# Two transformer blocks in fp32 by split products: order of the odd mixer, weight splits ahead of the square, places of a shift product and of a skew store

## The reference, cut to what matters

```python
def odd_mixer(h, w_in, w_out, ..., glu_w):
    q, k, v, gate, u = jnp.split(h @ w_in, ...)
    r = retention(rotary(q), rotary(k), v)                 # 4 heads, decay by distance
    r = rmsnorm(r) * jax.nn.silu(gate)
    y = jax.nn.gelu(s5_ssm(u, ...))                        # a state space scan over time
    ga, gb = jnp.split(y @ glu_w, 2, axis=-1)
    y = ga * jax.nn.sigmoid(gb)
    return jnp.concatenate([r, y], axis=-1) @ w_out

def conv_ffn(h, w_in, conv_w, conv_b, w_out):
    val, gate = jnp.split(h @ w_in, 2, axis=-1)
    gate = causal_conv_of_3_taps(gate, conv_w) + conv_b
    return (jax.nn.gelu(gate) * val) @ w_out
```

## Time and profile before

| what | value |
|---|---|
| median of three runs | 3336.36 us |
| the profiled execution | 3337.56 us |
| its span in the trace | 3335.8 us |
| TensorE matmul busy | 3213.4 us, 96% of the span |
| VectorE, ScalarE, GpSimd busy | 1816.6, 1182.0, 1014.5 us |
| mean granted clock of TensorE | 0.986 |

### The profile page before, as it was taken

The page is one execution under the profiler, slowest core; times in us unless marked ns, Lnnn a source line. Parts: engine busy times, 40 slices in busy tenths (PEclk is TensorE's granted clock), DMA queues, the critical chain, the costliest instruction groups (busy, mean ns, idle before and its releaser), DMA issues.

```text
span 3335.8 us, 40175 instructions
## 1 busy us (share of the span) xinstructions
PE 3213.4 (96%) x14573; PEld 2571.0 (77%) x14573; DVE 1816.6 (54%) x2464; ACT 1182.0 (35%) x1787; POOL 1014.5 (30%) x722
## 2 busy tenths in 40 slices
PE   6999999999999999999999998999999999899998
PEld 5888866778888888866778887776788777778887
DVE  5454465565446443465555544445776767375443
ACT  3222244432223222345332222454433342343332
POOL 3994000059911810000069800000699000021000
PEclk9999999999999999999999999999999999999999
DMA  6664332156634633321156633211566344243332
GB/s 217 208 207 134 99 107 71 57 167 205 208 103 124 205 109 94 101 73 52 57 183 206 201 93 111 63 51 57 174 204 200 93 124 102 63 134 99 101 89 94
DMA packets 576073, 420.42 MB, mean 126 GB/s; under 512 B 29238, under 2 KB 536197, under 8 KB 574809
## 3 DMA queue, kind: packets, MB, share of 16 engines
q1 hardware_dynamic: 535332, 284.78, 29.0%
q0 software_dynamic: 35456, 124.01, 12.0%
q10 hardware_dynamic: 5172, 10.17, 0.9%
HBM read 413.10 MB, written 8.68 MB: 126 GB/s over the span
## 4 chain that ended last, share of the span: by engine, by line
PE 85%; DVE 9%; ACT 3%; issue 1%; DMA 1%; ACTq 0%; SPq 0%; DVEq 0%
PE bank L326 25%; PE bank L328 24%; PE bank L327 24%; PE bank L1482 2%; PE bank L1510 2%; DVE w_lo L307 2%; ACT w_hi L290 1%; DVE tmp L451 1%; PE bank L1496 1%; DVE h_lo L461 1%; PE bank L432 1%; DVE w_lo L298 1%; PE bank L358 1%; PE bank L360 1%; PE bank L359 1%
## 5 line engine op out<-in xcount | busy, mean ns | idle before, releaser
L326 PE MATMUL bank<-h_hi,w_hi 128*128 128x512 f32 x2656 | 1050.3, 395 | 26.6 <-DVE w_lo L307 8.0
L328 PE MATMUL bank<-h_hi,w_lo 128*128 128x512 f32 x2656 | 1039.4, 391 | 0.0
L327 PE MATMUL bank<-h_lo,w_hi 128*128 128x512 f32 x2656 | 1038.9, 391 | 0.0
L307 DVE TENSOR_TENSOR w_lo<-raw,w_hi 128x1024 fp32r<-128x1024 f32 x438 | 635.6, 1451 | 568.2 <-ACT w_hi L290 561.7
L290 ACT ACTIVATE w_hi<-raw 128x1024 fp32r<-128x1024 f32 x438 | 462.1, 1055 | 650.0 <-PE bank L328 649.7
L326 PEld LDWEIGHTS bank<-h_hi,w_hi 128*128 128x128 f32 x2656 | 499.7, 188 | 152.5 <-issue 20.9
L328 PEld LDWEIGHTS bank<-h_hi,w_lo 128*128 128x128 f32 x2656 | 499.9, 188 | 108.1 <-issue 1.3
L327 PEld LDWEIGHTS bank<-h_lo,w_hi 128*128 128x128 f32 x2656 | 500.4, 188 | 103.0 <-issue 2.0
L732 POOL TENSOR_TENSOR mod_acc<-mod_acc,mod_w 128x1024 f32<-128x1024 f32 x168 | 439.2, 2614 | 14.7
L326 PE MATMUL bank<-hid_hi,w_hi 128*128 128x512 f32 x1056 | 413.3, 391 | 5.8 <-DVE w_lo L307 5.3
L328 PE MATMUL bank<-hid_hi,w_lo 128*128 128x512 f32 x1056 | 411.0, 389 | 0.0
(11 more groups left out here) (402 smaller groups left out, 3291.2 us busy)
## 6 DMA issues: line engine op xcount, KB each, us to landing
raw<-in_ffn_w_gu SPq DMA_DIRECT2D x176, 512.0 KB, 4.4
mod_w<-in_w_ada POOLq DMA_DIRECT2D x128, 512.0 KB, 3.7
mod_w<-in_mod_w POOLq DMA_DIRECT2D x96, 512.0 KB, 4.0
raw<-in_ffn_w_in SPq DMA_DIRECT2D x88, 512.0 KB, 3.6
raw<-in_ffn_w_down SPq DMA_DIRECT2D x64, 512.0 KB, 3.6
raw<-in_w_in SPq DMA_DIRECT2D x34, 512.0 KB, 3.5
raw<-in_ffn_w_out SPq DMA_DIRECT2D x32, 512.0 KB, 3.6
raw<-in_ffn_w_down SPq DMA_DIRECT2D x32, 384.0 KB, 3.3
```

The costliest lines, as they stand in the source:

```text
L307: loop(nc.vector.tensor_tensor(w_lo[:, u % 2, :], raw[:, u % 2, :], w_hi[:, u % 2, :].bitcast(F32), ALU.subtract), "split_lo", times)
L326: nc.tensor.matmul(dst, a_hi, b_hi, start=start, stop=False)
L327: nc.tensor.matmul(dst, a_hi, b_lo, start=False, stop=False)
L328: return nc.tensor.matmul(dst, a_lo, b_hi, start=False, stop=stop)
```

## The change

It has six parts. (1) In the output loops the split of the next unit stands ahead of the square on both engines, except in the last turn. (2) Where the phase before is a mixer, the second shift product and the first half's sum are made in `convert_dve`, behind the reciprocal of the norm, and not between the last two tiles of the output loop. (3) In the first turn of the two feed-forwards with convolution, each split stands one place earlier, up to the second turn, which is written out singly for that. (4) The skew store is issued behind the first exps of m1's attention. (5) In the odd mixer the gates' units go to other banks, the scores of heads 0 and 1 come ahead of unit 13, unit 15 comes behind the head sums; the scores of heads 2 and 3 come between the two halves of the state's outputs; all four gelus come behind the head root, in tiles of their own (`y_hi`, `y_lo`); `scan(25, STEPS)` comes behind `decay(0)` and `decay(1)`. (6) The GLU units use four pairs of banks, and the first two output units are interleaved so that the last two merged tiles are needed later.

```diff
 # convert_dve
+            if PHASES[PHASES.index(key) - 1][0] != "f":
+                fold_product(dve, key, 1, turn.dve - 1)
+                fold_sum(dve, key, 0)
             fold_sum(dve, key, 1)
 # act_out (dve_out likewise, with split_lo_loop behind the add to x and ahead of the add of the square)
+                        early = q == parts - 1 and not (isinstance(i, int) and i == 3)
+                        if early:
+                            split_hi_loop(act, i, per, mm * parts + q, times)
                         if q == parts - 1:
                             act.wait_ge(sg.sem("x_ready"), i * 2 + (x0 + mm + 1))
...
-                        split_hi_loop(act, i, per, mm * parts + q, times)
+                        if not early:
+                            split_hi_loop(act, i, per, mm * parts + q, times)
 # dve_out, last turn
-                        if nxt is not None and isinstance(i, int) and i == 3 and k == per - 2:
+                        if nxt is not None and isinstance(i, int) and i == 3 and k == per - 2 and parts > 1:
                             fold_product(dve, nxt, 1, u0 + 4 * per + LOOK - 1)
                             fold_sum(dve, nxt, 0)
 # act_ffn, dve_ffn, kind "conv" (begun: second tile of turn 0)
-                        if not begun:
+                        if not begun and not (jj == 0 and key in LAZY and isinstance(i, int) and i == 1):
                             split_hi_loop(act, i, 4, 2 * jj, times)
...
-                        if not begun:
-                            split_hi_loop(act, i, 4, 2 * jj + 1, times)
+                        split_hi_loop(act, i, 4, 2 * jj + (2 if begun else 1), times)
 # pe_odd
             unit(12)
-            unit(13)
             wait(pe, "values_read", (key, 3))
             wait(pe, "taps_read", key)
             scores(0)
+            unit(13)
             retain(0)
             retain(1)
+            unit(14)
             outputs(0)
-            wait(pe, "ret_read", (key, 0))
-            unit(14)
+            scores(1)
             outputs(1)
-            wait(pe, "ret_read", (key, 1))
-            unit(15)
-            scores(1)
+            wait(pe, "decayed", (key, 3))
+            heads_sum(pe, key, 0, 2)
             retain(2)
             retain(3)
-            heads_sum(pe, key)
+            heads_sum(pe, key, 2, 4)
             after_hidden(pe)
+            unit(15)
             wait(pe, "state_read", (key, 3))
             heads_spread(pe, key, ODD_SPREAD)
...
+                for mm, kts in ((0, range(6)), (1, range(4)), (0, range(6, 8)), (1, range(4, 8))):
 # dve_odd
-            scan(25, STEPS)
             wait(dve, "decay_loaded", key)
             wait(dve, "taps_stored", key)
             decay(0)
             decay(1)
+            scan(25, STEPS)
             split_lo(dve)
             gate_head(0)
             gate_head(1)
             split_lo(dve)
+            decay(2)
+            decay(3)
             skip(0)
             skip(1)
-            split_lo(dve)
-            decay(2)
-            decay(3)
...
+            gate_head(2)
+            heads_invert(dve, key)
             skip(2)
             skip(3)
...
+            for t in range(4):
+                low(t)
+            split_lo(dve)
```

More of the change, by code:

```diff
@@ L1435, in emit @@
         g[0] += TQ * ROW
-        o_sig = place("o_sig", [P, TQ, S], F32, g)
+        y_hi = place("y_hi", [P, TQ, S], F32R, g)
+        y_lo = place("y_lo", [P, TQ, S], F32R, [tmp_at])
+        o_sig = place("o_sig", [P, TQ, S], F32, [group + 8 * NF * S])
         o_r = o_gate
@@ L1902, in act_mla @@
             v0 = u0 + FRONT + 5
+            if l == 0:
+                wait(act, "bias_stored", "all")
+                src = bass.AP(scratch.tensor, 0, [[640, 12], [0, P], [1, 640]])
+                dst = bass.AP(skewed.tensor, 0, [[P * 641, 12], [641, P], [1, 640]])
+                done(act.dma_start(dst, src), "bias_skewed", "all", 16)
             for h in range(HEADS):
@@ L2685, in retain @@
             def retain(h):
-                wait(pe, "decayed", (key, h))
-                wait(pe, "proj_read", (key, 12 + h))
+                wait(pe, "decayed", (key, max(h, 3 * (h // 2))))
+                if h == 1:
+                    wait(pe, "proj_read", (key, 13))
                 if h >= 2:
@@ L2742, in pe_odd @@
                 for m in range(2):
-                    bank = 2 * (n % 2) + m
+                    bank = ODD_GLU[n][m]
+                    if n == 0:
+                        wait(pe, "ret_read", (key, 2 + m))
                     if n == 1:
                         wait(pe, "r_ready", (key, 3))
-                    if n >= 2:
+                    if n == 3:
                         wait(pe, "glu_done", (key, m))
@@ L2749, in pe_odd @@
                         c = slice(kt * 2 * P + m * P, kt * 2 * P + (m + 1) * P)
-                        ins = mm3(psum[bank][:, :], w_hi[:, s, c], w_lo[:, s, c], h_hi[:, kt, :], h_lo[:, kt, :], kt == 0,
+                        ins = mm3(psum[bank][:, :], w_hi[:, s, c], w_lo[:, s, c], y_hi[:, kt, :], y_lo[:, kt, :], kt == 0,
                                   kt == 3)
@@ L2753, in pe_odd, with begin @@
                         unit_end(ins)
-            pe_out(pe, key, KT, lambda kt: o_m_hi[:, kt, :], lambda kt: o_m_lo[:, kt, :],
-                   lambda pe, kt: wait(pe, "merged", (key, kt)), key == final)
+            u0 = turn.pe
+            def begin(pe):
+                for mm, kts in ((0, range(6)), (1, range(4)), (0, range(6, 8)), (1, range(4, 8))):
+                    s = (u0 + mm) % 2
+                    pe.wait_ge(sg.sem("split_lo"), u0 + mm + 1)
+                    for kt in kts:
+                        wait(pe, "merged", (key, kt))
+                        c = slice(kt * P, (kt + 1) * P)
+                        ins = mm3(psum[5 + mm][:, :], w_hi[:, s, c], w_lo[:, s, c], o_m_hi[:, kt, :], o_m_lo[:, kt, :],
+                                  kt == 0, kt == KT - 1)
+                        if kt == KT - 1:
+                            done(ins, "unit_used")
+            pe_out(pe, key, KT, lambda kt: o_m_hi[:, kt, :], lambda kt: o_m_lo[:, kt, :], lambda pe, kt: None, key == final,
+                   begin)
         def act_odd(act, key):
@@ L2845, in state @@
                      "state_read", (key, u))
-            for u in range(2):
+            unit(14)
+            for u in range(4):
                 state(u)
-            unit(14)
-            for u in range(2, 4):
-                state(u)
-            unit(15)
-            gelu(0)
-            gelu(1)
             for h in range(2, 4):
@@ L2856, in act_odd @@
                 heads_square(act, key, h, psum[h % 2][:, :])
-            gelu(2)
-            gelu(3)
+            root_table(act)
             heads_root(act, key)
+            for t in range(4):
+                gelu(t)
+            unit(15)
             for h in range(4):
@@ L2945, in low @@
                 wait(dve, "y_hi", (key, t))
-                done(nc.vector.tensor_tensor(h_lo[:, t, :], o_u[:, t, :], h_hi[:, t, :].bitcast(F32), ALU.subtract),
+                done(nc.vector.tensor_tensor(y_lo[:, t, :], o_u[:, t, :], y_hi[:, t, :].bitcast(F32), ALU.subtract),
                      "y_lo", (key, t))
```

67 lines of the change are left out of this document (36 added, 31 removed).

## The result

The changed kernel takes 3286.41 us (median of four runs, 3284.77 to 3289.14), the kernel before 3336.41 beside it: ratio 0.9852, 95% interval 0.9835 to 0.9869. Five more runs later gave 0.9848 (0.9831 to 0.9865). The profiled execution took 3284.77 us with a span of 3283.0.

A forecast was written before the change was run, and what follows sets the result against it. TensorE, busy 96% of the span, was taken as the bound, leaving its idle and low-clock time to win. Terms of 19.6, 6.9, 7.2, 3.6 and 2.4 us summed to 39.7, giving 3297 us, range 3289 to 3316.

The forecast's parts named there:

- odd mixer, late part: End of the second output unit: 16.3 us of waits and 4.9 of low clock go, 1.6 come new; gain 19.6 us.
- second shift product: Four waits for the square following a mixer: 1.35 us each, plus 1.5 us of low clock into f7; 6.9 us.
- convolution's first turns: First turns of f7 and f9: earlier splits remove most of a 2.3 us wait and 1.5 of clock each; 7.2 us.
- skew store: m1: moving the store ends its delay of a weight load, making m1 as long as m4; 3.6 us.
- early splits, f7's output: f7's output: a split 2.3 us earlier hides three waits for a split behind the square; 2.4 us.
- Elsewhere, 60 places in ten phases, a loop runs without waits and nothing changes: Output loops outside f7's: splits ahead of the square were claimed to gain nothing there.
- The clock: TensorE at 1.2 GHz behind waits: 4.9 us won back in the odd mixer, 1.5 at f7's square, 1.5 per convolution turn.
- the walk's 95 us: Odd mixer, unit 11's end to the second output unit's: new order followed instruction by instruction, 115.0 us falling to 95.
- its tightest place: Odd mixer's GLU: the third head's read of its bank at 2867.0, wanted by TensorE at 2867.4; 0.4 us to spare.
- rival C: Output loops: VectorE waits for ScalarE's rounding, each of 60 tiles 0.9 us late; slower, 3353 us; chance 3%.
- rival B: Convolution's splits lose against GpSimd and the odd mixer's tight chain is 4 us late; 3310 us; chance 14%.
- Rival A: Low clock stays: new short waits make 1.2 GHz stretches appear elsewhere; 3308 us; chance 20%.

The follow-up runs named there:

- product alone: Kernel before with only the second shift product and first half's sum moved behind the reciprocal where a mixer precedes: 3328.73 us, ratio 0.9969.
- convolution alone: Kernel before with only the earlier splits in the first turn of f7 and f9: 3333.81 us, ratio 0.9991.
- taken back: Changed kernel with the output loops' splits put behind the square again: 3303.23 us, ratio 0.9905.
- early splits alone: Kernel before with only the next unit's split ahead of the square in output loops, except the last turn: 3324.89 us, ratio 0.9959.
- skew store alone: Kernel before with only the skew store moved behind the first exps of m1's attention: 3332.57 us, ratio 0.9979.
- odd mixer alone: Kernel before with only the odd mixer's new order, GLU banks and interleaved output units included: 3319.55 us, ratio 0.9949.
- without GpSimd's last product: Changed kernel without GpSimd's last multiplication in f7, leaving 128 rows of one modulation vector unscaled: 3290.81 us, ratio 0.9840.
- changed, two more moves: Changed kernel with low part and split ahead of angles and sines at f7's output, head 3's gate ahead of second GLU split: 3280.44 us.

## Why the prediction was wrong

The mechanisms were right and the direction too; the sum was short. Waits first, in stretches cut at the same matmuls and free of the clock; predicted without its clock parts.

| term | predicted | measured | from |
|---|---|---|---|
| odd mixer, late part | 14.7 | 14.1 | both traces |
| second shift product | 5.4 | 7.1 | product alone |
| convolution's first turns | 4.2 | 4.9 | both traces |
| its cost at f7's output | 0 | -1.5 | convolution alone |
| skew store | 1.9 | 1.9 | both traces |
| early splits, f7's output | 2.4 | 3.3 | taken back |
| early splits, third unit of m1 and m4 | 0 | 4.0 | both traces |

That is 28.6 predicted, 33.8 by this table, 32.0 in the trace.

**The step that failed** is "Elsewhere, 60 places in ten phases, a loop runs without waits and nothing changes", and with it the term of 2.4 us for the early splits. I had read the list of waits by stretch for f7's output only. In the row for the whole span the split of the loops stood with 17.4 us in 21 waits; the earlier trace rows account for 6.7 us in 7 of them, and f9's first turn for 2.3. The two places of 2.0 us in m1 and m4 were in what was left over. Part (1), forecast at 2.4 us, is worth some 14 us alone and 16 in the whole, of which some 11 us are waits in either case: the 4.0 us of m1 and m4, 3.3 in f7's output, and the rest at the squares (alone) or in o8 (in the whole). Those 2.0 us in o8, behind the odd mixer's stretch, are waited for only in the new order, and the prediction took it for granted that they are not, because it walked that order with the early split already in it.

**The second shift product** was mis-sized, 7.1 in place of 5.4. I had left 0.1 and 0.15 us of each wait over; in fact each went whole, and the four stretches are shorter by 1.7 to 1.9 us where the wait was 1.6.

**The clock** was mis-sized. My terms hold 11.1 us of it (4.9 odd mixer, 1.5 shift product, 3.0 convolution, and 1.7 in the skew store). In the profiled execution of before, the late stretch of the odd mixer has 8.5 us of it by its list of clock levels: I had missed the stretch of 6.8 us in the heads' spread, where TensorE's small matmuls ran at 0.51, and which I dated as 6.1 us in both orders. The stretch, then the spread in before and in the changed kernel:

```profile
2869.70:2876.60 6.90, 5.37 (x25) 5.40 (x26) 1.86 (x4) 2.35 (x4) 0.00 (x0) 0.51 0.00 0
```
```profile
2871.23 6.35 PE L432 MATMUL bank<-ident,stat 128*128 128x128 f32 x32 [3.27 <-DVE stat L2118]
```
```profile
2834.08 3.73 PE L433 MATMUL bank<-ident,stat 128*128 128x128 f32 x32
```

Those 2.6 us are most of what the walk's 95 us had too much against 92.4.

How much the clock takes varies from run to run, so only means say something. Mean granted clock, and (1 - clock) x time as its cost:

| kernel | runs | mean us | clock | cost, us |
|---|---|---|---|---|
| before | 49 | 3337.5 | 0.9851 | 49.7 |
| early splits alone | 5 | 3323.7 | 0.9858 | 47.2 |
| product alone | 11 | 3327.3 | 0.9863 | 45.7 |
| convolution alone | 11 | 3333.7 | 0.9860 | 46.7 |
| skew store alone | 12 | 3331.0 | 0.9868 | 43.9 |
| odd mixer alone | 5 | 3321.4 | 0.9870 | 43.2 |
| changed | 9 | 3288.9 | 0.9896 | 34.4 |
| without GpSimd's last product | 5 | 3288.2 | 0.9892 | 35.5 |
| part (1) taken back | 6 | 3304.2 | 0.9892 | 35.8 |
| changed, two more moves | 5 | 3281.2 | 0.9916 | 27.6 |

The cost includes the 5 us behind the last matmul in every run, and the 6.8 us at the start in those runs whose record has them; how many do is not known but for the profiled ones (the second trace of the changed kernel and the one without GpSimd's last product). So a mean can be wrong by some us.

Over these, the change gives back 15 us by the clock where I had 11, and 33 us by waits where I had 28.6: 48.6 us by the means. The gains of the five parts alone, 13.8, 10.2, 3.8, 6.5 and 16.1 us by the means, add up to 50.4, so they do not need each other beyond what this measurement can tell, and that is not much: the interval of each ratio is 2 to 3 per mille, 6 to 11 us, wide. (The odd mixer's part does need part (1), by the 2.0 us in o8.)

**The range** reached down to 3289 us "(all upper bounds)". The upper bounds add up to 43.2 us (21, 8, 7.6, 3.6, 3), which gives 3294: even by its own bounds the prediction could not reach the 3286.41 us measured.

**Right** were the odd mixer's walk (92.4 us for 95, no wait but for 0.8 us ahead of the outputs, forecast at 1.1), except at its tightest place: the bank of head 3, forecast with 0.4 us to spare, cost the 1.4 us wait. Waits for `sq` at the sums fell to 1.3 us, where 2 were forecast. The clock's mean, 0.9896 over nine runs, fell just short of the 0.99 that was to show it right. Right too were m1's stretch, the absence of waits in f7's and f9's second turns, and the fall of rival C: in the output loops TensorE waits for no tile. In f9 the split started at 2938.92, 0.23 us ahead of GpSimd's sum (VectorE, then GpSimd):

```profile
2938.92 1.23 DVE L308 TENSOR_TENSOR w_lo<-raw,w_hi 128x1024 fp32r<-128x1024 f32 x1
```
```profile
2939.15 3.25 POOL L736 TENSOR_TENSOR mod_acc<-mod_acc,mod_w 128x1024 f32<-128x1024 f32 x1
```

Against the earlier trace rows it is now GpSimd that takes 3.25 us in place of 2.39. The race of rival B was won here by 0.23 us, which is luck as much as forecast, and lost at a place that I had not looked at, f7's output. **Rival A** has a part: of the profiles with the new order, the first of the changed kernel, that of the odd mixer alone and that of the two more moves have no low clock in its late stretch, the changed kernel's second trace has 3.4 us' worth, part (1) taken back 1.7, and the kernel without GpSimd's last product 8.5.

**Open.** Why a given short wait is followed by the lower clock in one run and not in the next. At 453 and 1443 us in the trace of before, behind waits that no part touches, the stretch is there in some of the traces and missing in others. The 15 us rest on means of records that are given to 0.001, 3.3 us a step; no kernel here held the waits fixed and changed the clock.

## What to carry to other kernels

Take the row with the largest total of the whole-span list and give every one of its waits a place before you write that the rest is nothing: what is left over after the places you know is the part you have missed. When an engine has background work whose length you don't change, and you speed up another beside it, look at where its last instruction will now lie. Price the lower clock from several traces, not from one, as a sum over the kernel with its spread.

## What was not expected of the hardware

The same kernel, in two traces with the same waits, spent 25.5 and 37.3 us' worth at the lower clock (6.8 more are only in the record of the second), and its nine runs span 3284.8 to 3297.0 us; before's 49 span 3327.8 to 3347.1. A VectorE operation of 0.69 us took 2.63 with GpSimd's sum beside it and ended 0.55 us behind that sum. The list of granted clocks can begin late: in nine of the eleven traces it begins at 57 to 60 us, and the matmuls of 128x512 ahead of that already run at half the rate, 0.43 us apart. In the two where it begins at 42 to 44 us the same stretch is listed as low clock, and it costs nothing more: from the first matmul to the 1901st it took 445.4 us in the changed kernel's second trace and 446.7 in its first.
